# The attention probabilities of places 3 to 8: divided by GpSimd in 16 pieces and turned by VectorE in place of TensorE

## What is computed

```
s = einsum(q, k of up to 3 blocks) * HEAD_DIM ** -0.5 + bias     # 4 heads; bias by relative position
m = max(max(s), sink);  p = exp(s - m)
denom = sum(p) + exp(sink - m)
o = einsum(p / denom, v)
x = x + concat([o, ssd, mlstm]) @ w_out
h2 = rmsnorm(x);  logits = h2 @ router                           # then the experts
```

## Time and profile before

| engine | busy us | share of the span |
|---|---|---|
| TensorE (PE) | 2273.0 | 98% |
| VectorE (DVE) | 1239.2 | 53% |
| ScalarE (ACT) | 622.8 | 27% |
| GpSimd (POOL) | 542.8 | 23% |

### The profile page before, as it was taken

The page is one execution under the profiler, slowest core; times in us unless marked ns, Lnnn a source line. Parts: engine busy times, 40 slices in busy tenths (PEclk is TensorE's granted clock), DMA queues, the critical chain, the costliest instruction groups (busy, mean ns, idle before and its releaser), DMA issues.

```text
span 2317.1 us, 33010 instructions
## 1 busy us (share of the span) xinstructions
PE 2273.0 (98%) x12766; PEld 1613.8 (70%) x12766; DVE 1239.2 (53%) x2399; ACT 622.8 (27%) x1445; POOL 542.8 (23%) x552
## 2 busy tenths in 40 slices
PE   8999999999999999999999999999999999999998
PEld 6556587874556778887775665878755567888776
DVE  3554466586647344555236434765865463455542
ACT  3221233464332111111132212335633421111111
POOL 1003454144211111111110034532432111111111
PEclk9999999999999999999999999999999999999999
DMA  4002132221127988878530111312212279888883
GB/s 155 21 25 68 55 122 74 74 91 56 74 73 254 348 302 292 299 264 284 148 120 21 37 55 59 119 60 82 83 55 82 82 274 343 300 290 274 284 295 83
DMA packets 149653, 352.16 MB, mean 152 GB/s; under 512 B 9941, under 2 KB 38105, under 8 KB 149498
## 3 DMA queue, kind: packets, MB, share of 16 engines
q1 hardware_dynamic: 134234, 308.11, 37.1%
q0 software_dynamic: 15264, 41.95, 7.4%
HBM read 307.75 MB, written 42.28 MB: 151 GB/s over the span
## 4 chain that ended last, share of the span: by engine, by line
PE 93%; DVE 4%; DMA 1%; ACT 1%; issue 1%; POOL 0%; SPq 0%; DVEq 0%; ACTq 0%; POOLq 0%
PE ps L1842 89%; PE ps L2127 1%; PE ps L2188 1%; DVE HT L1784 1%; PE ps L1861 1%; DVE TMP L1248 1%; DMA HT<-h_sample,idxs 0%; PE ps L1894 0%; DVE HT L1248 0%; PE ps L2139 0%; DVE TMP L1257 0%; ACT SCR L1051 0%; DMA MID<-w_in 0%; DVE SCR L1248 0%; POOL SCR L753 0%
## 5 line engine op out<-in xcount | busy, mean ns | idle before, releaser
L1842 PE MATMUL ps<-MID,HT 128*128 128x512 f32 (+3 forms) x2560 | 694.2, 491 | 4.8 <-DMA MID<-w_in 3.0
L1842 PEld LDWEIGHTS ps<-HT,MID 128*128 128x128 f32 x4096 | 557.2, 191 | 16.4 <-issue 15.4
L1842 PE MATMUL ps<-HT,MID 128*128 128x160 f32 (+1 forms) x4096 | 560.5, 299 | 1.0 <-DVE HT L1248 0.9
L1842 PEld LDWEIGHTS ps<-MID,HT 128*128 128x128 f32 (+1 forms) x2560 | 293.7, 157 | 248.3 <-issue 207.7
L1842 PE MATMUL ps<-RING,HT 128*128 128x256 f32 (+2 forms) x1760 | 395.8, 392 | 1.7 <-DVE RING L1252 1.3
L1842 PEld LDWEIGHTS ps<-RING,HT 128*128 128x128 f32 (+1 forms) x1760 | 310.7, 189 | 83.5 <-issue 40.7
L1842 PE MATMUL ps<-HT,RING 128*128 128x512 f32 (+1 forms) x960 | 350.0, 522 | 0.0
L1842 PEld LDWEIGHTS ps<-HT,RING 128*128 128x128 f32 x960 | 180.2, 190 | 157.8 <-issue 149.8
L1784 DVE STREAM_TRANSPOSE HT<-HT 32x256 f32<-32x256 f32 x576 | 251.0, 436 | 18.3
L1257 DVE SCALAR_TENSOR_TENSOR HT<-HT,ps 128x160 f32<-128x160 f32 (+1 forms) x128 | 40.9, 319 | 397.1 <-ACT HT L1210 395.1
L850 POOL DMA_INDIRECT y_prompt<-SCR,idxp x32 | 50.5, 1578 | 583.1 <-ACT SCR L1220 562.2
(11 more groups left out here) (268 smaller groups left out, 2177.2 us busy)
## 6 DMA issues: line engine op xcount, KB each, us to landing
MID<-w_gate SPq DMA_DIRECT2D x32, 2048.0 KB, 9.4
MID<-w_up SPq DMA_DIRECT2D x32, 2048.0 KB, 15.0
MID<-w_down SPq DMA_DIRECT2D x32, 2048.0 KB, 16.2
RING<-w_in SPq DMA_DIRECT2D x20, 1024.0 KB, 5.3
SCR<-cs_rows SPq DMA_DIRECT2D x20, 1024.0 KB, 5.2
MID<-w_out SPq DMA_DIRECT2D x8, 1024.0 KB, 6.4
y_sample<-RING SPq DMA_DIRECT2D x16, 512.0 KB, 2.6
h_sample<-HT SPq DMA_DIRECT2D x16, 512.0 KB, 2.6
```

What stands on the lines that cost most here:

```text
L1842: return pe.matmul(out, a, b, start=start, stop=stop)
```

## The change

Places 0, 1, 2 and 9 (`BY_ROWS`) keep the old way. For places 3 to 8:

- `scores` reads the keys with the four groups of 32 of each block outermost, and PSC is laid out by key group, head, key block (`attn_shift` and `attn_exps` work on strided views).
- `attn_scale` is 16 instructions on 32 partitions each (384 elements, or 256 with two key blocks). Each takes the rows of one quadrant of 32 partitions and one key group, and writes to the quadrant of that key group in a new tile PB. They follow one another without a wait.
- VectorE's new `turn_p` transposes PB in blocks of 32 x 32 into PT: one instruction of 1536 elements, or four of 256. It stands in VectorE's queue behind `attn_shift(n + 2, 1)` and ahead of `take_x(n)`. `keep_p` of ScalarE and `turn_p` of TensorE go for these places.
- The bias is kept in forward order by key group: the load goes to another tile (STAGE) in the mLSTM stage, and GpSimd reverses it with four copies in layer 0. For `BY_ROWS` places the bias sum in `attn_shift` becomes two instructions of half the size. Two of the four loads of `w_out` move from chunks 3 and 4 of the mLSTM stage to chunks 6 and 7. Two semaphores are merged into one.

```diff
+BY_ROWS = (0, 1, 2, NC - 1)
-        PSC = [SCR[:, 1536 * b:1536 * (b + 1)].rearrange("p (h k) -> p h k", h=AH) for b in range(2)]
+        PSCF = [SCR[:, 1536 * b:1536 * (b + 1)] for b in range(2)]
+        PSC = [a.rearrange("p (b h x) -> p b h x", b=4, h=AH) for a in PSCF]
+        PSN = [a.rearrange("p (h k) -> p h k", h=AH) for a in PSCF]
+        PB = PBF.rearrange("p (a h x) -> p a h x", a=4, h=AH)
@@ SyncE, loads of the mLSTM stage
-                        if c in (3, 4):
-                            k = 2 * c - 4
+                        if layer == 0 and c == 2:
+                            sp.wait_ge(hot_loaded, 32)
+                            sp.wait_ge(wk_made, 2 * len(STEPS))
+                            sp.dma_start(STAGE, bass.AP(tensor=btab.tensor, ...)).then_inc(hot_loaded, 16)
+                        if c in (6, 7):
+                            if layer == 0 and c == 6:
+                                sp.wait_ge(md_masked, 2 * 6 + 1)
+                            k = 2 * c - 10
@@ GpSimd, attn_scale(n)
-                        v = PSC[n % 2][:, :, 0:nk * P]
-                        link(pool.tensor_tensor(v, v, ADEN[n % 2].unsqueeze(2).to_broadcast([P, AH, nk * P]), ALU.mult), pn_made)
+                        v = PSC[n % 2][:, :, :, 0:w]
+                        if n >= 4:
+                            pool.wait_ge(p_placed, n - 3)
+                        for a in range(4):
+                            at = slice(32 * a, 32 * a + 32)
+                            for b in range(4):
+                                link(pool.tensor_tensor(PB[32 * b:32 * b + 32, a, :, 0:w], v[at, b],
+                                                        ADEN[n % 2][at].unsqueeze(2).to_broadcast([32, AH, w]), ALU.mult),
+                                     pn_made if a == b == 3 else pool_chain, wait=a == b == 3)
@@ VectorE, attn_shift(n, j)
-                        tt(v, ps[:, b:b + 2, 0:nk * P], bia[:, j:AH:2, b1 - nk * P:b1][:, :, ::-1], ALU.add, s_read)
+                        if n in BY_ROWS:
+                            for q in range(2):
+                                h = j + 2 * q
+                                link(dve.tensor_tensor(PSN[n % 2][:, h, 0:nk * P]..., ps[:, b + q, 0:nk * P]..., bia[:, h, ...], ALU.add),
+                                     s_read if q else dve_chain)
+                        else:
+                            v = PSC[n % 2][:, :, j:AH:2, 0:w].rearrange("p b h x -> p h b x")
+                            tt(v, ps[:, b:b + 2, 0:nk * P].rearrange("p h (b x) -> p h b x", b=4), bia[:, j:AH:2, :, at:at + w], ALU.add, s_read)
...
+                    def turn_p(n):
+                        nk, c0 = attn_keys(ORDER[n])
+                        dve.wait_ge(pn_made, n + 1)
+                        dve.wait_ge(o_made, n)
+                        out = PT.rearrange("p (h k a j) -> p a h k j", h=AH, k=3, a=4)[:, :, :, 0:nk, :]
+                        if nk == 3:
+                            link(dve.transpose(out.rearrange("p a h k j -> p a (h k) j"), PB.rearrange("p a h (k i) -> p a (h k) i", k=3)), p_placed)
+                            return
+                        for a in range(4):
+                            turned = link(dve.transpose(out[:, a], PB[:, a, :, 0:32 * nk]...), p_placed if a == 3 else dve_chain, wait=a == 3)
@@ VectorE, round n
                             attn_shift(n + 2, 1)
+                        if n + 1 not in BY_ROWS:
+                            turn_p(n + 1)
                         take_x(n)
                         keep_h2(n - 1, 1)
@@ TensorE, round n (each of the four calls of turn_p)
-                        if n + 1 < NC:
+                        if n + 1 in BY_ROWS:
                             turn_p(n + 1, 0)
```

More of the change, by code:

```diff
@@ L604, in _ @@
                     ring_load(10)
-                    sp.wait_ge(mrow_stored, 32)
+                    sp.wait_ge(scratch_stored, 48)
                     sp.wait_ge(y_made, NC)
@@ L761, in _ @@
                             ml_mask(c + 2, 1)
+                        if layer == 0 and c == 3:
+                            pool.wait_ge(hot_loaded, 48)
+                            for h in range(AH):
+                                link(pool.tensor_copy(bia[:, h].rearrange("p b (k i) -> p b k i", k=3),
+                                                      STAGE[:, h][:, ::-1].rearrange("p (k b i) -> p b k i", k=3, b=4)))
                         if c == NC:
@@ L1093, in attn_exps @@
                         for h in range(h0, h1):
-                            v = PSC[n % 2][:, h, 0:nk * P]
+                            v = PSC[n % 2][:, :, h, 0:32 * nk] if n not in BY_ROWS else PSN[n % 2][:, h, 0:nk * P]
                             link(act.activation(v, v, ACT.Exp, bias=ANMX[n % 2][:, h:h + 1], accum_out=ADEN[n % 2][:, h:h + 1]))
@@ L1568, in attn_shift @@
                             tt(e, pr("sink"), neg, ALU.add, s_shift)
+                    def turn_p(n):
[5 more added lines that the diff above has]
+                            link(dve.transpose(out.rearrange("p a h k j -> p a (h k) j"), PB.rearrange("p a h (k i) -> p a (h k) i", k=3)), p_placed)
+                            return
+                        for a in range(4):
+                            turned = link(dve.transpose(out[:, a], PB[:, a, :, 0:32 * nk].rearrange("p h (k i) -> p h k i", k=nk)),
+                                          p_placed if a == 3 else dve_chain, wait=a == 3)
                     def attn_den(n):
@@ L2116, in scores @@
                         for g in range(2):
-                            last = mm(ps[:, b + g, 0:nk * P], QT[64 * g:64 * g + 64, j, c * P:(c + 1) * P],
-                                      KT[64 * g:64 * g + 64, c0 * P:(c0 + nk) * P])
+                            keys = KT[64 * g:64 * g + 64, c0 * P:(c0 + nk) * P]
+                            if n not in BY_ROWS:
+                                keys = keys.rearrange("p (k b i) -> p b k i", b=4, i=32)
+                            last = mm(ps[:, b + g, 0:nk * P], QT[64 * g:64 * g + 64, j, c * P:(c + 1) * P], keys)
                         last.then_inc(s_made, 1)
@@ L2123, in turn_p @@
                         pe.wait_ge(pn_made, n + 1)
-                        if AH * n + h >= 2:
-                            pe.wait_ge(p_kept, AH * n + h - 1)
+                        i = AH * BY_ROWS.index(n) + h
+                        if i >= 2:
+                            pe.wait_ge(p_kept, i - 1)
                         for b in range(nk):
-                            last = pe.transpose(ps[:, 6 + h % 2, b * P:(b + 1) * P], PSC[n % 2][:, h, b * P:(b + 1) * P], ident)
+                            last = pe.transpose(ps[:, 6 + h % 2, b * P:(b + 1) * P], PSN[n % 2][:, h, b * P:(b + 1) * P], ident)
                         last.then_inc(p_turned, 1)
@@ L2148, in turn_y @@
                             nk, c0 = attn_keys(at)
-                            pe.wait_ge(p_kept, AH * (n + 1))
+                            if n in BY_ROWS:
+                                pe.wait_ge(p_kept, AH * (BY_ROWS.index(n) + 1))
+                            else:
+                                pe.wait_ge(p_placed, n - 2)
                             pe.wait_ge(yt_copied, 3 * n + 2)
```

53 lines of the change are left out of this document (31 added, 22 removed).

## The result

| | median us | lowest to highest | runs | ratio to before, 95% interval |
|---|---|---|---|---|
| before | 2318.28 | 2316.87 to 2318.97 | 19 | |
| after | 2321.72 | 2319.34 to 2324.03 | 19 | 1.0015, 1.0009 to 1.0021 |

The change costs 3.4 us. Forecast were 2324 us, with 0.58 on slower and 0.30 on no change.

A forecast was written before the change was run, and what follows sets the result against it. The prediction took TensorE's queue (98% busy) to bound the kernel. Its terms, -13.9 + 16.9 + 1.1 + 2.8 = +6.9 us, took the profiled 2318.55 to 2325.4, or 2324 us for a median, range 2312 to 2342.

The forecast's parts named there:

- the waits of the two-block rounds: Rounds 6 and 7: TensorE's router product waits 1.08 and 1.27 us for VectorE, with four small transposes taking 1.74 us.
- TensorE's transposes: Attention rounds: TensorE loses its transposes of places 3 to 8, 6.96 us a layer, 13.9 us in both.
- router product waits: Attention rounds: TensorE's router product waits for keep_h2 behind VectorE's transpose, 8.45 us a layer, 16.9 in both.
- start of the stage: Ahead of the attention loop: split sums of places 0 to 2 on VectorE cost 0.57 us a layer, 1.1 in both.
- collision in round 3: VectorE's ml_output, slowed by GpSimd's pieces at round 2's end, makes scores(5, 1) wait 1.4 us, 2.8 in both layers.
- The turn: VectorE's transpose ahead of take_x and keep_h2: 1.77 us for 1536 elements, making the router product wait 1.66 us in round 2.
- The cover: GpSimd's place 4 ends its pieces at 590.4, VectorE wants them at 593.7: 3.3 us to spare.
- Overlapping pieces: Rival: GpSimd's pieces run four at a time, 16 in about 3.5 us, the 2.8 us go: 2321.3 us; chance 0.17.
- GpSimd as the bound: Rival: at 1.25 us a piece GpSimd overruns its cover, costing some 10 us a layer: 2344 us; chance 0.18.
- A gain that stays: Rival: VectorE's transpose is hidden by keep_h2's slack, TensorE keeps its 13.9 us less the start: 2304.5 us; chance 0.11.
- A fast transpose: Rival: VectorE's transpose takes 1.14 us, the wait of four rounds falls by 0.63 each in both layers: 2319 us; chance 0.08.

The follow-up runs named there:

- e_behind: Changed kernel with VectorE's turn of place n+1 moved behind take_x, keep_h2 and keep_y(n+1,1), TensorE's list unchanged; 2320.0 us, ratio 1.0007.
- e_split: Kernel before with only the sums of scores and bias of places 0, 1, 2 and 9 split into two instructions; 2319.9 us, ratio 1.0006.
- e_one: Changed kernel with GpSimd's 16 pieces of places 3 to 8 replaced by one product in place, output not computed; 2320.98 us, ratio 1.0011.
- e_best: As e_behind, with TensorE's turn_y(n+1,2) behind the folding product (places 3 to 8) and VectorE's squares ahead of keep_y(n+1,2); 2311.49 us, ratio 0.9973.
- e_short: Changed kernel with VectorE's turn cut to one block of 32 columns in places 3 to 8, output not computed; 2306.5 us, ratio 0.995.
- e_late: As e_behind, with TensorE's turn_y(n+1,2) moved four products and the folding product later for places 3 to 8; 2329.1 us, ratio 1.0045.
- e_best_split: As e_best, with the last part of ml_output moved to round 3 behind attn_shift(n+2,0) on VectorE; 2313.62 us, ratio 0.998.
- e_mid: As e_best, but VectorE's squares stay behind keep_y(n+1,2) as in the changed kernel; 2315.68 us, ratio 0.9989.

## Why the prediction was right, term by term

The mechanism, its place and the sign of the sum were as forecast; the sum was +6.9 us and +3.4 were measured. The forecast time of 2324 us comes nearer to the measured 2321.72 than the sums do, by chance: the median of the kernel before was 1.0 higher beside these runs than the 2317.24 that the forecast started from. With half the size the result falls on the other side of the 0.2% line (4.6 us) than the 0.58 given to slower. What was mis-sized are the waits of the two-block rounds and the collision. Four terms, taken from stretches of TensorE's timeline in layer 0:

| term, both layers | forecast | measured, layer 0 | both |
|---|---|---|---|
| TensorE's transposes | -13.9 | -7.04 | -14.1 |
| router product waits | +16.9 | 7.56 | +15.1 |
| start of the stage | +1.1 | 0.56 | +1.1 |
| collision in round 3 | +2.8 | 0.70 | +1.4 |
| sum | +6.9 | | +3.5 |

- **TensorE's saving.** From `turn_qk` to the router product round 2 takes 574.94 - 561.04 = 13.90 us before and 574.41 - 561.83 = 12.58 in e_behind, where the router product waits for nobody: 1.32 saved, as forecast. Round 5 gives 1.32 too, and rounds 6 and 7, from their first `scores`, 0.88 each (forecast 0.84): 4 x 1.32 + 2 x 0.88 = 7.04 a layer. Nothing is left for the keys read in groups.
- **The turn.** The one large instruction was priced at 1.77 us and took 1.78. In the changed kernel the same stretch of round 2 takes 575.10 - 560.91 = 14.19, so the wait costs 1.61, against 1.66; the 0.05 are the hand-over, 575.04 to 575.10, for which the forecast had 0.11. The profile's bracket says 1.54, because it counts from the modelled end of the product before, and a product that does not wait starts 0.06 ahead of that end (574.94 and 573.12 + 1.88 in the kernel before). Round 5 costs 1.08, forecast 1.12. The two-block turns were mis-sized: four instructions of 436 ns were added up to 1.74, but four that do not wait for each other take 1.42, and so rounds 6 and 7 cost 0.72 and 0.92 instead of 1.08 and 1.27.
- **The start.** 0.57 forecast, 0.56 measured; e_split shows that it is the split sums.
- **The collision.** The mechanism is shown by e_one; its size was mis-sized by half, 0.70 a layer in place of 1.4. Counted from `turn_qk` of round 2, the bias sum comes 1.23 us later than before (24.96 to 26.19), forecast 2.05. `ml_output` lost 1.96 where 2.75 were forecast, and the square gained 1.44 in place of 0.7, of which VectorE then lost 0.43 waiting for the fold. Another 0.29 come from `keep_y(n + 1, 2)`, which TensorE paces and which is later by what the router wait exceeds the saving; the forecast gave this shift to TensorE (0.34) and not to VectorE.
- **GpSimd.** 16 pieces take 14.6 to 15.1 us, 0.91 to 0.95 a piece, forecast 0.87. The cover was 1.94 us in round 2 and 3.0 in round 3, forecast 3.3. `root_out` behind them came 6.2 us later than before (586.46 to 592.65), forecast 4. They stay hidden in the changed kernel. They are not hidden in e_best, where the root behind them reaches TensorE over ScalarE's queue.
- **The rivals.** Overlapping pieces: refuted. A piece takes 0.82 us and the next starts 0.08 behind its end, also where the source quadrant changes (the fourth of place 3 ends at 559.11, the fifth starts at 559.19). The rule of the Trainium skill named there (GPSIMD Engine Reference, section Instruction dispatch), that a core goes on to the next instruction without waiting for the others, does not show in this kernel's pieces; the measurement decides. GpSimd as the bound: refuted by e_one. A gain that stays: only e_short and the re-ordered kernels have it; the limit of 0.16 us named for it is 0.11 by the forecast's own numbers, since the gap of 0.04 behind the turn counts too. A fast transpose: refuted by the 1.78 us.

## What to carry to other kernels

Work moved off the bounding engine is gained only if its new place delays nothing that this engine asks for next, the product that reads the moved work included: look for the idle time of the receiving queue and put the work where that idle time is, not where its input becomes ready. When a product is moved later on one queue, move its reader on the other queue too, or everything behind the reader pays. After each wait that goes, list the waits again: here the waits went from the router product (14.2 us) to the attention product (12.8 in e_behind), then to the next round's scores (13.0 in e_late), then to the fold (4.4 in e_best_split), before they were gone.

## What the hardware showed that was not expected

- Where in GpSimd's instruction a VectorE instruction comes decides what it pays. The square of 128x384 takes 0.56 us alone; in the traces of before and of the runs it ends either 0.56 after its start or 0.41 to 0.42 behind the end of the GpSimd instruction it starts in, whichever is later. The 2.75 us product ended at 579.20 before and the square at 579.61 (2.00 us long), at 579.14 and 579.55 in e_one (1.43 long), a piece at 577.62 and the square at 578.03 in e_short (0.85 long). In the changed kernel the square of round 2 starts at 577.78, between two pieces, takes 0.56, and the piece behind it takes longer instead:

```profile
576.94 0.82 POOL L772 TENSOR_TENSOR HT<-SCR,small 32x384 f32<-32x384 f32 x1
...
577.83 1.19 POOL L772 TENSOR_TENSOR HT<-SCR,small 32x384 f32<-32x384 f32 x1
```

The small instruction of `ml_output` (0.17 us before) starts 0.01 us into a piece and takes 0.83, ending 0.03 behind that piece.
- An instruction with one SBUF tensor as input stood too: the scaling of 128x64 (0.26 us before) took 0.48 in e_best, 0.57 in e_short and 0.68 in e_late beside the pieces.
- GpSimd's 16 pieces hold the same elements as one product of 2.75 us and take 14.6: each uses 32 of 128 partitions, and they come one after the other.
- TensorE's granted clock fell from 1.00 to 0.50 behind waits of 1.81 to 4.55 us in e_late, and behind one of two waits of 2.85 in e_mid, so that a wait cost about 1.6 to 2.7 us more than its length. Behind the waits of 1.54 in the changed kernel it stayed at 1.00.
